# Rotary swap on VectorE instead of TensorE, and the first norm's root taken out of the projections' input

## The chip, the cores and the metric

The kernel runs on one core of one Trainium2 chip. The metric is the device time of one launch in microseconds (us). Before the change three runs took 2022.5, 2027.2 and 2033.6 us; the median, 2027.2 us, is the time before.

## The reference, cut to what matters

Two transformer blocks are computed on 512 tokens of width 1024 in fp32. What bears on the change:

```python
def rmsnorm(x, g):
    y = xf * lax.rsqrt(jnp.mean(xf * xf, axis=-1, keepdims=True) + NORM_EPS)
    return y * g
...
rot = jnp.concatenate([x1 * cos - x2 * sin, x2 * cos + x1 * sin], axis=-1)      # apply_rope
...
xn = rmsnorm(x, norm_mix_g[l])                                                  # the first norm
proj = jnp.einsum('bsd,de->bse', xn, w_in[l])
q_lat, kv_lat, k_rope, dq, dk, dv, gate_pre = jnp.split(proj, split_idx, axis=-1)
...                       # latents normed and projected up, rope on q_pe, k_pe, dq, dk; two attentions
gates = jax.nn.sigmoid(gate_pre + b_gate[l])
merged = (g_mla * jnp.einsum('bse,ed->bsd', o_mla, w_branch_mla[l])
          + g_diff * jnp.einsum('bse,ed->bsd', o_diff, w_branch_diff[l]))
```

After that come an output projection and a gated feed-forward network of hidden width 2816, then the second block: feed-forward, a mixer with two more attentions (its own rope on dq, dk, iq, ik), feed-forward.

## The kernel before

Activations lie feature-major: a tile is 128 features (partitions) by 512 tokens. `X` holds the 8 tiles of the residual. All large weights come from memory as one stream of 311 chunks of 128x1024 fp32 values. SyncE loads chunk n into `RAW[n % 3]`, ScalarE (ACT) rounds it to `HI` (`split_hi`, L967), VectorE (DVE) subtracts to get `LO` (`split_lo`, L1357), and TensorE (PE) multiplies with the pairs (`split_product`, L379 to L381): for each block of 128 features three matmuls, high by high, high by low and low by high. One chunk is thus 24 matmuls of 512 columns. ACT may split chunk n+3 only when chunk n is used, so two chunks are ready ahead of PE.

Each engine runs its own program, written by hand, and waits on semaphores. The order in an engine's program is the order in the code: in step j of a projection PE multiplies chunk j, ACT and DVE first split chunk j+2 and then do what belongs to step j. There is no planner.

The parts that the change touches:

- The start. `norm(0)` needs all of `X`: squares (ACT, L981) are summed (DVE, L1392), PE sums over partitions with matmuls against ones (`norm_sums`, L424 and L428), ACT takes the root, DVE inverts and spreads it, PE transposes it into PSUM bank 6 (`norm_spread`, L447). Then for each tile DVE scales (`scaled`, L1445), ACT rounds to `XH` (L1006) and DVE subtracts to `XL` (L1457). `behind` lets PE multiply the first two chunks tile by tile as these come. `keep_warm` (L395) runs matmuls of no use before and between.
- `project_in1`, 14 chunks: 3 tiles of q latents (`LATQ`), 2 of kv latents (`LATK`), `KR`, 4 of `DQ`, 4 of `DK`. ACT copies each out of PSUM (L1067). Two small norms of the latents run between (`norm_sums(1)` ahead of chunk 5, `norm_spread(1)` ahead of 7, `norm_sums(2)` ahead of 8, `norm_spread(2)` ahead of 11). DVE also makes the angles of the rotary tables (`angles`, L1478 to L1484).
- Rotary. For a tile, `rotate` (L462) is an fp32 matmul with a signed permutation matrix from `SQC`, which swaps the halves; DVE multiplies that by sine (L1522), the tile by cosine (L1524) and adds (L1539). There are 18: 9 in `project_in1`, 2 with the `uq` and `uk` chunks, 7 in `project_in2` (one of them `rotate_misc`).
- After `project_in1` PE waits until all 14 tiles are copied (`all_released`) and multiplies the 4 chunks `dv1`, then differential attention, `uq`, `uk`, `uv`, the second attention.
- `merge(0)`: for each of 8 output tiles two gate chunks and one branch chunk. ACT takes the sigmoid of the gates from PSUM (L1220). In the first step DVE normalizes the differential output (`diff_norm`, L1807 and L1811), PE transposes both attention outputs (`turn`, L774), ACT rounds and DVE subtracts them (L1766, L1762).

Of the kernel before, what the change touches and what calls it, by code (L numbers as in the profile page):

```python
# [7 lines left out]
F32 = mybir.dt.float32  # L8
# [7 lines left out]
P = 128  # L16
# [27 lines left out]
SQUARES = ("ident", "ones", "halves", "rot_a", "rot_p", "rot_i", "rot_m", "causal", "chunked")  # L44
NSQ = len(SQUARES)

# [16 lines left out]
def build(nc, wst, ada, xT, cols_d, squares_d, pos1_d, pos2_d, lams_d, out):  # L63
    ctx = ExitStack()
    with ctx:
# [18 lines left out]
        WARM = [(4, 1, 2), None, None, (1, 1, 2), (1, 1, 1), (1, 1, 2), (1, 1, 2)]  # L84
# [25 lines left out]
        SM2 = at("SM2", 206.5, [P, 48])  # L110
        A0 = 118
# [83 lines left out]
        FSTD, FR, FV = SM3[:, 0:8], SM3[:, 8:16], SM3[:, 16:24]  # L195
        G_BOTH = SM2[:, 40:48]
# [10 lines left out]
        NTB = np.cumsum([0] + [n[0] for n in NORMS]).tolist()  # L207
        SAB = np.cumsum([0] + [n[0] - 1 for n in NORMS]).tolist()
# [31 lines left out]
        ROT_BASE = {"in1": 0, "uq": len(ROT1), "in2": len(ROT1) + 2}  # L240
        rot_src = {}
# [64 lines left out]
        def _(pool):  # L306
            pool.dma_start(T[:, 0, :].bitcast(I32), pos1_d.partition_broadcast(P)).then_inc(sem("pos_loaded"), 16)
# [51 lines left out]
        def _(pe):  # L359
# [31 lines left out]

            def keep_warm(n):
# [46 lines left out]
            def norm_spread(k):  # L439

                pe.wait_ge(sem("expanded"), k + 1)
                if k:

                    pe.wait_ge(sem("normed"), NTB[k])
# [19 lines left out]
            def token_major(n0, nchunks, tiles_per, width, moving, banks, rotations):  # L464


                for j in range(nchunks):
                    w = chunk(n0 + j, 0, 0)
                    for b in range(NB):
                        if j == 0 and b == 2:  # L470
                            pe.wait_ge(sem("rot_read"), rotations)
# [27 lines left out]
            def project_in2():  # L499
# [31 lines left out]
                def rotation(k):  # L531
                    q = ROT_BASE["in2"] + ROT2.index(k)
                    if IN2[k][0] == "rope":
                        pe.wait_ge(sem("in_copied"), e0 + k + 1)
                    else:
                        pe.wait_ge(sem("hnormed"), NRM2.index(k) + 1)

                    if q > ROT_BASE["in2"]:
                        pe.wait_ge(sem("rot_read"), q)
                    if q == ROT_BASE["in2"] + 2:  # L540
                        pe.wait_ge(sem("values_copied"), 1)
                    rotate(q, IN2[k][1], "rot_m" if IN2[k][0] == "misc" else IN2[k][3], 5)

                def turn_values():

                    pe.wait_ge(sem("in_copied"), e0 + 3)
                    pe.wait_ge(sem("rot_read"), ROT_BASE["in2"] + 2)
# [5 lines left out]
                for j in range(IN2_STEPS):  # L553
# [7 lines left out]
                    turning = [k for k in ROT2 if rot_at(IN2, k) == j]  # L561
                    if turning:
                        amid[4] = lambda: rotation(turning[0])
# [8 lines left out]
                    if j == len(IN2):  # L572

                        pe.wait_ge(sem("in_copied"), e0 + len(IN2))
                        pe.wait_ge(sem("rot_read"), ROT_BASE["in2"] + len(ROT2))
# [50 lines left out]
            def project_in1():  # L626

                n0 = FIRST["in1"]
                for j in range(len(IN1) + 2):
                    if j - 2 in ROT1:  # L630
                        q = ROT1.index(j - 2)
                        pe.wait_ge(sem("in_copied"), j - 1)
                        if q >= 2:
                            pe.wait_ge(sem("rot_read"), q - 1)
                        rotate(q, IN1[j - 2][1], IN1[j - 2][3], 4 + q % 2)
# [8 lines left out]
                    if j == 0:  # L644
                        behind(0, n0, (0, 1))
                    elif 2 <= j < len(IN1):
# [3 lines left out]
                        used(split_product(PS[:, j % 4, :], w, range(8), range(8), (XH, XL)))  # L650
                released["in_copied"] += len(IN1)
# [232 lines left out]
            pe.wait_ge(sem("squares_loaded"), 16)  # L884
            norm(0)
            project_in1()
            all_released()

            pe.wait_ge(sem("normed"), NTB[3])
            token_major(FIRST["dv1"], 4, 2, 512, (XH, XL), DV_BANKS, len(ROT1))  # L890
# [14 lines left out]
            for m in range(4):  # L905
# [3 lines left out]
                if m in (1, 2):  # L909
                    r = m - 1  # L910
                    pe.wait_ge(sem("proj_copied"), 5 + r)
                    rotate(ROT_BASE["uq"] + r, Y[:, r, :], "rot_p", 6 + r)
            used(ins)
            token_major(FIRST["uv"], 1, 2, 512, (LKH, LKL), UV_BANKS, ROT_BASE["uq"] + 2)
# [35 lines left out]
        def _(act):  # L950
# [51 lines left out]
            def high(k, t):  # L1002
                g, oh = NORMS[k][3:5]
                act.wait_ge(sem("normed"), NTB[k] + t + 1)
# [26 lines left out]
            def token_copies(n0, nchunks, dest, width, banks):  # L1031
# [7 lines left out]
                for b in range(NB):  # L1039
                    A(dest[:, b, :], PS[:, banks[b], 0:width], ACT.Copy).then_inc(sem("v_copied"), 1)  # L1040
# [1127 lines left out]
```

## Time and profile before

| | |
|---|---|
| runs timed | 2022.5, 2027.2, 2033.6 us |
| profiled execution | span 2022.8 us from first to last instruction; its page has no other time of its own |
| PE busy | 1987.2 us (98%) |
| DVE busy | 1001.7 us (50%) |
| ACT busy | 713.8 us (35%) |
| memory read | 204 MB, 102 GB/s over the span |
| mean granted TensorE clock | 0.991 |

Busy time of an engine is the time in which it executes something, not the time at its peak rate. A row of the timeline gives start, duration, engine, line and operation, and in brackets how long the engine sat idle before it and what ended that. The chain of waits is the path that ended last, walked back from the last instruction. An fp32 matmul of 512 columns shows as two records, one of rounded operands as one.

### The profile page before, as it was taken

The numbers are of one execution on the slowest core, as the hardware profiler recorded it, in microseconds if no ns is written. First come the engines' busy times: TensorE is split into PE (matmuls) and PEld (weight loads), VectorE is DVE, ScalarE is ACT, GpSimd is POOL, SyncE is SP. The second block draws the span as 40 slices with busy tenths as digits, with TensorE's granted clock in tenths as the row PEclk, the third lists the DMA queues.
The fourth block names the chain that finished last, engine by engine and source line by source line (L and its number), as shares of the span: only waits on it lengthen the run. The fifth ranks groups of instructions, "written<-read, shape, count | busy, mean of one in ns | idle before, by whom it ended". The sixth has DMA issues, their size and how long they took to land.

```text
span 2022.8 us, 25559 instructions
## 1 busy us (share of the span) xinstructions
PE 1987.2 (98%) x9174; PEld 1591.1 (79%) x9182; DVE 1001.7 (50%) x1525; ACT 713.8 (35%) x1210; POOL 77.9 (4%) x113
## 2 busy tenths in 40 slices
PE   6999999999999999999999999999999999999999
PEld 4866778878888888788888878767777878888887
DVE  5655654467656533543334344767834653333322
ACT  4334742233222222422232223445544433232221
POOL 0010000001111000000000010400000000000000
PEclk9998999999999999999999999999999999999999
DMA  5220114455766533233333322211111223333332
GB/s 174 82 67 11 43 63 131 131 174 194 220 205 218 171 104 104 78 105 95 102 93 102 106 83 84 74 52 53 42 42 32 94 74 106 102 93 94 103 104 93
DMA packets 57513, 207.36 MB, mean 103 GB/s; under 512 B 6448, under 2 KB 6576, under 8 KB 57440
## 3 DMA queue, kind: packets, MB, share of 16 engines
q1 hardware_dynamic: 46800, 167.94, 26.5%
q0 software_dynamic: 10640, 38.44, 6.1%
q8 instruction: 47, 0.77, 0.2%
q14 instruction: 26, 0.21, 0.0%
HBM read 204.23 MB, written 2.10 MB: 102 GB/s over the span
## 4 chain that ended last, share of the span: by engine, by line
PE 94%; DVE 3%; ACT 2%; issue 1%; DMA 1%; SPq 0%; DVEq 0%; ACTq 0%
PE PS L379 27%; PE PS L381 26%; PE PS L380 26%; PE PS L726 3%; PE PS L760 2%; PE PS L665 1%; PE PS L744 1%; PE PS L462 1%; DMA SQC<-squares 1%; PE PS L854 1%; PE PS L395 1%; PE PS L687 1%; PE PS L527 1%; PE PS L496 1%; DVE BIAS L1679 0%
## 5 line engine op out<-in xcount | busy, mean ns | idle before, releaser
L1357 DVE TENSOR_TENSOR LO<-RAW,HI 128x1024 fp32r<-128x1024 f32 x311 | 383.6, 1234 | 547.4 <-ACT HI L967 546.0
L379 PE MATMUL PS<-XH,HI 128*128 128x512 f32 x1552 | 626.5, 404 | 4.6 <-ACT GATE_F L1161 2.1
L381 PE MATMUL PS<-XH,LO 128*128 128x512 f32 x1552 | 605.8, 390 | 0.0
L380 PE MATMUL PS<-XL,HI 128*128 128x512 f32 x1552 | 605.1, 390 | 0.0
L967 ACT ACTIVATE HI<-RAW 128x1024 fp32r<-128x1024 f32 x311 | 328.1, 1056 | 558.2 <-PE PS L381 541.0
L379 PEld LDWEIGHTS PS<-XH,HI 128*128 128x128 f32 x1552 | 292.2, 188 | 82.3 <-issue 19.0
L381 PEld LDWEIGHTS PS<-XH,LO 128*128 128x128 f32 x1552 | 291.6, 188 | 62.1
L380 PEld LDWEIGHTS PS<-XL,HI 128*128 128x128 f32 x1552 | 292.3, 188 | 56.7 <-issue 2.6
L379 PE MATMUL PS<-HIDH,HI 128*128 128x512 f32 x528 | 205.4, 389 | 0.0
L380 PE MATMUL PS<-HIDL,HI 128*128 128x512 f32 x528 | 205.4, 389 | 0.0
L381 PE MATMUL PS<-HIDH,LO 128*128 128x512 f32 x528 | 205.4, 389 | 0.0
L379 PEld LDWEIGHTS PS<-HIDH,HI 128*128 128x128 f32 x528 | 99.1, 188 | 20.6
L381 PEld LDWEIGHTS PS<-HIDH,LO 128*128 128x128 f32 x528 | 99.1, 188 | 20.6
L380 PEld LDWEIGHTS PS<-HIDL,HI 128*128 128x128 f32 x528 | 99.1, 188 | 20.5
L1255 ACT ACTIVATE T<-PS 128x512 f32<-128x512 f32 x45 | 26.9, 598 | 165.4 <-PE PS L381 165.2
L1884 DVE TENSOR_TENSOR Y<-T,PS 128x512 f32<-128x512 f32 x45 | 31.0, 688 | 95.6 <-PE PS L381 95.6
L1505 DVE SCALAR_TENSOR_TENSOR ACC<-ADA,SM,ACC 128x1024 f32<-128x1024 f32 x57 | 73.0, 1281 | 10.3 <-DMA ADA<-ada 9.8
L1177 ACT ACTIVATE PT<-PS 128x128 f32<-128x128 f32 (+1 forms) x96 | 42.1, 438 | 83.8 <-PE PS L744 83.7
L1730 DVE TENSOR_REDUCE SM<-PS 128x1 f32<-128x128 f32 (+1 forms) x96 | 46.8, 489 | 32.1 <-PE PS L731 12.3
L1187 ACT ACTIVATE P<-PS,SM 128x128 f32<-128x128 f32 (+1 forms) x96 | 50.5, 526 | 25.0 <-DVE SM L1730 24.1
L316 POOL DMA_DIRECT2D ADA<-ada x70 | 36.9, 528 | 526.9 <-DVE ACC L1503 252.6
L379 PE MATMUL PS<-OTH,HI 128*128 128x512 f32 x128 | 50.1, 391 | 0.4 <-DVE OTL L1762 0.4
(323 smaller groups left out, 2085.2 us busy)
## 6 DMA issues: line engine op xcount, KB each, us to landing
RAW<-weights SPq DMA_DIRECT2D x311, 512.0 KB, 3.5
ADA<-ada POOLq DMA_DIRECT2D x72, 512.0 KB, 4.5
X<-x_in SPq DMA_DIRECT2D x4, 512.0 KB, 8.5
y_out<-X SPq DMA_DIRECT2D x8, 256.0 KB, 4.7
SQC<-squares SPq DMA_DIRECT2D x1, 576.0 KB, 11.9
T<-positions POOLq DMA_DIRECT2D x1, 256.0 KB, 5.7
POS<-positions POOLq DMA_DIRECT2D x1, 256.0 KB, 3.5
LAMS<-lambdas POOLq DMA_DIRECT2D x1, 128.0 KB, 7.0
```

What stands on the lines that cost most here:

```text
L316: pool.dma_start(ADA[j][:], ada[2 * i + (j + 2)]).then_inc(sem(f"ada{j}"), 16)
L379: mm(bank, a, moving[0][:, t, :], start=start, stop=False)
L380: mm(bank, a, moving[1][:, t, :], start=False, stop=False)
L381: ins = mm(bank, z, moving[0][:, t, :], start=False, stop=stop)
L726: mm(PS[:, u % 3, 0:n], at_["q"](h, i), at_["k"](h, n), start=True, stop=False)
L760: ins = mm(PS[:, 5 + v % 2, 0:at_["dv"]], at_["PT"][v % 2][:, kb * P:(kb + 1) * P], at_["v"](kb, h), start=kb == 0, stop=kb == i)
L967: A(HI[n0 % 3][:], RAW[n0 % 3][:], ACT.Copy).then_inc(sem("hi_ready"), 1)
L1177: A(at_["PT"][v % 2][:, 0:n], PS[:, 3 + v % 2, 0:n], ACT.Copy).then_inc(sem("pt_copied"), 1)
L1187: A(at_["P"][u % 3][:, 0:n], PS[:, u % 3, 0:n], ACT.Exp, bias=NMX[:, u % 4:u % 4 + 1], accum_out=RSU[:, u % 4:u % 4 + 1]).then_inc(sem("pr ...
L1357: V.tensor_tensor(LO[n0 % 3][:], RAW[n0 % 3][:], HI[n0 % 3][:].bitcast(F32), ALU.subtract)\
L1505: V.scalar_tensor_tensor(out=ACC[:], in0=ADA[j][:], scalar=CND[:, kt:kt + 1], in1=ACC[:], op0=ALU.mult, op1=ALU.add).then_inc(sem("ada_add ...
L1730: V.tensor_reduce(NMX[:, u % 4:u % 4 + 1], PS[:, u % 3, 0:n], AX, ALU.max, negate=True)\
```

## The change

Three things change.

1. Rotary swap. The permutation matmul goes. DVE's `stream_shuffle` swaps lanes within each group of 32 partitions, from SBUF to SBUF; the sign is in the sine table now (`_freq`). A rope on DVE is thus four operations for three, and its first one reads the copied tile, no longer PSUM. The four permutation matrices leave `SQC`, which shrinks from 9 to 5 squares; `R0` takes their place in SBUF.
2. First norm. `XH` and `XL` are made from `X` times the gain, without the root. The squares follow, the sums are taken by PE after the first two chunks and the root is spread after chunk 2. DVE copies it to `R0`, and multiplies each tile by it as it takes the tile out of PSUM, which ACT did before. The `dv1` rows are scaled in ACT's copy (`NR0`). In `merge(0)` DVE multiplies each gate tile by `R0`, and ACT takes the sigmoid of that. `lambdas`, a handful of small DVE operations, moves from ahead of the projection to its step 3.
3. Loads. SyncE issues `X` and the first three chunks in turns, then `SQC`; GpSimd waits for the last part of `X` before it issues its own. `warm_up` runs five matmuls on a cleared tile at the start, and the seven useless matmuls of norm 0 go.

```diff
-        WARM = [(4, 1, 2), None, None, (1, 1, 2), (1, 1, 1), (1, 1, 2), (1, 1, 2)]
+        WARM = [None, None, None, (1, 1, 2), (1, 1, 1), (1, 1, 2), (1, 1, 2)]
@@ sync
             for t in range(4):
                 sp.dma_start(X[:, 2 * t:2 * t + 2, :], xT[:, 2 * t:2 * t + 2, :]).then_inc(sem(f"x_loaded{t}"), 16)
+                if t < 3:
+                    sp.dma_start(RAW[t][:], wst[t]).then_inc(sem(f"raw{t}"), 16)
             sp.dma_start(SQC[:], squares_d).then_inc(sem("squares_loaded"), 16)
-            for j in range(3):
-                sp.dma_start(RAW[j][:], wst[j]).then_inc(sem(f"raw{j}"), 16)
@@ gpsimd
+            pool.wait_ge(sem("x_loaded3"), 16)
@@ tensor
-            def rotate(q, src, perm, bank):
-                mm(PS[:, bank, :], SQV[perm], src, start=True, stop=True).then_inc(sem("rot_mm"), 1)
...
                     if j == 0:
                         behind(0, n0, (0, 1))
+                        pe.wait_ge(sem("squares_loaded"), 16)
+                        norm_sums(0)
...
+                    if j == 2:
+                        norm_spread(0)
@@ scalar
+                A(XH[:, t, :], X[:, t, :], ACT.Copy, scale=col("g_mix", t)).then_inc(sem("split_hi"), 1)
+                if t in (1, 3):
+                    split_hi(t // 2 - 2)
+            for t in range(DT):
                 square(0, t)
-            split_hi(-2)
-            split_hi(-1)
-            norm(0, first=DT)
             project_in1()
@@ vector, rope
-                v.wait_ge(sem("rot_mm"), q + 1)
-                ins = V.tensor_tensor(T[rows, 0, :], PS[rows, bank, :], tab[rows, 1, :], ALU.mult)
-                ins.then_inc(sem("rot_read"), 1)
-                link(V.tensor_tensor(T[rows, 1, :], dst[rows, :], tab[rows, 0, :], ALU.mult))
-                return T
+                V.stream_shuffle(T[rows, 0, :], src[rows, :], SWAP[swap]).then_inc(sem("swapped"), 1)
+                swaps[0] += 1
+                link(V.tensor_tensor(T[rows, 1, :], src[rows, :], tab[rows, 0, :], ALU.mult))
+                v.wait_ge(sem("swapped"), swaps[0])
+                link(V.tensor_tensor(T[rows, 0, :], T[rows, 0, :], tab[rows, 1, :], ALU.mult))
@@ vector, project_in1
+                    if j == 0:
+                        roots_of(0)
+                    if j == 1:
+                        v.wait_ge(sem("rstd"), 1)
+                        V.tensor_copy(R0[:], PS[:, 6, :]).then_inc(sem("normed"), 1)
+                        v.wait_ge(sem("normed"), 1)
+                    if 1 <= j <= len(IN1):
+                        v.wait_ge(sem("chunk_used"), n0 + j)
+                        kind = IN1[j - 1]
+                        V.scalar_tensor_tensor(out=kind[1], in0=PS[:, (j - 1) % 4, :],
+                                               scalar=kind[4] if len(kind) > 4 else 1.0, in1=R0[:], op0=ALU.mult,
+                                               op1=ALU.mult).then_inc(sem("in_copied"), 1)
+                    if j == 3:
+                        lambdas()
@@ vector, merge
                             split_lo(n0 + 3 * j + g, 6, i)
+                            v.wait_ge(sem("chunk_used"), 6 * i + (n0 + 3 * j + g + 1))
+                            V.tensor_tensor(T[:, g, :], PS[:, 4 * j + g, :], R0[:], ALU.mult)\
+                                .then_inc(sem("gate_raw"), 1)
                         if isinstance(i, int) and j == 0:
                             diff_norm()
```

How the order moves on DVE in one step of `project_in1`, the one that rotates the first tile of `DQ` (step 8). Before:

```order
L1357 TENSOR_TENSOR LO_59<-RAW_53,HI_56 128x1024 [waits hi_ready]
L1522 TENSOR_TENSOR T<-PS,TAB_A_83 128x512 [waits rot_mm]
L1524 TENSOR_TENSOR T<-DQ,TAB_A_83 128x512
L1539 TENSOR_TENSOR DQ<-T 128x512 [waits rot_read,dve_link]
L1445 SCALAR_TENSOR_TENSOR Y<-LATQ,CO,PS 128x512 [waits split_hi,split_lo,rstd,rotated]
L1457 TENSOR_TENSOR LQL<-Y,LQH 128x512 [waits split_hi]
```

And after:

```order
L1340 TENSOR_TENSOR LO_59<-RAW_53,HI_56 128x1024 [waits hi_ready]
L1526 SCALAR_TENSOR_TENSOR DQ<-PS,R_75 128x512 [waits chunk_used]
L1506 STREAM_SHUFFLE T<-DQ 128x512 [waits in_copied]
L1508 TENSOR_TENSOR T<-DQ,TAB_A_84 128x512
L1510 TENSOR_TENSOR T<-T,TAB_A_84 128x512 [waits swapped,dve_link]
L1538 TENSOR_TENSOR DQ<-T 128x512 [waits dve_link]
L1429 SCALAR_TENSOR_TENSOR Y<-LATQ,CO,PS 128x512 [waits split_hi,split_lo,rstd,rotated]
L1441 TENSOR_TENSOR LQL<-Y,LQH 128x512 [waits split_hi]
```

The step gains the copy out of PSUM (L1526) and the shuffle (L1506); the copy waits for a chunk, and what follows stands behind it.

On DVE early in `project_in1`, after the change, from the split of chunk 3 to the split of chunk 4 (`R_75` is `R0`; before the change only the first row, the cast and the angles stand there):

```order
L1340 TENSOR_TENSOR LO_58<-RAW_52,HI_55 128x1024 [waits hi_ready]
L1521 COPY R_75<-PS 128x512 [waits rstd]
L1526 SCALAR_TENSOR_TENSOR LATQ<-PS,R_75 128x512 [waits chunk_used,normed]
L1559 CAST T<-T 128x512 [waits pos_loaded]
L1463 TENSOR_SCALAR Y<-T,CO 128x512 [waits dve_link]
L1464 TENSOR_SCALAR RB<-Y 128x512 [waits dve_link]
L1465 TENSOR_SCALAR RB<-RB 128x512 [waits dve_link]
L1467 SCALAR_TENSOR_TENSOR Y<-RB,Y 128x512 [waits dve_link] x3
L1469 TENSOR_SCALAR Y<-Y 128x512 [waits dve_link]
L1340 TENSOR_TENSOR LO_59<-RAW_53,HI_56 128x1024 [waits hi_ready]
```

The angles and the split of chunk 4 now stand behind a wait for the root (`rstd`), which PE spreads after chunk 2.

On DVE at the start of `merge(0)` before (`OTL` takes the low part of the turned attention outputs):

```order
L1357 TENSOR_TENSOR LO_59<-RAW_53,HI_56 128x1024 [waits hi_ready,g_sub_scaled]
L1357 TENSOR_TENSOR LO_60<-RAW_54,HI_57 128x1024 [waits hi_ready]
L1807 RECIPROCAL SM<-SM 128x16 [waits diff_std]
L1811 TENSOR_SCALAR OD<-OD,SM 128x128 [waits dve_link]
L1811 TENSOR_SCALAR OD<-OD,SM 128x128 x15
L1766 TENSOR_TENSOR OTL_101<-PS,OTH_100 128x512 [waits turned_hi] x4
```

And after:

```order
L1340 TENSOR_TENSOR LO_59<-RAW_53,HI_56 128x1024 [waits hi_ready,g_sub_scaled]
L1786 TENSOR_TENSOR T<-PS,R_75 128x512 [waits chunk_used]
L1340 TENSOR_TENSOR LO_60<-RAW_54,HI_57 128x1024 [waits hi_ready]
L1786 TENSOR_TENSOR T<-PS,R_75 128x512 [waits chunk_used]
L1817 RECIPROCAL SM<-SM 128x16 [waits diff_std]
L1821 TENSOR_SCALAR OD<-OD,SM 128x128 [waits dve_link]
L1821 TENSOR_SCALAR OD<-OD,SM 128x128 x15
L1773 TENSOR_TENSOR OTL_102<-PS,OTH_101 128x512 [waits turned_hi] x4
```

The normalization of the differential output stands behind both gate chunks now.

## Rows read from the trace of the kernel before

**Rows 1.** The page, busy time and share of each engine.
```profile
PE 1987.2 (98%) x9174; PEld 1591.1 (79%) x9182; DVE 1001.7 (50%) x1525; ACT 713.8 (35%) x1210; POOL 77.9 (4%) x113
```

**Rows 2.** The page, chain that ended last, shares by engine.
```profile
PE 94%; DVE 3%; ACT 2%; issue 1%; DMA 1%; SPq 0%; DVEq 0%; ACTq 0%
```

**Rows 3.** Timeline of the start: start us, duration us, engine, line, operation.
```profile
14.46 1.15 ACT L981 ACTIVATE SQ<-X 128x512 f32<-128x512 f32 x2 [1.41 <-DMA X<-x_in]
15.75 5.18 PE L395 MATMUL PS<-SQC 128*128 128x512 f32 x8 [15.75 <-DMA SQC<-squares]
...
18.28 1.06 ACT L967 ACTIVATE HI<-RAW 128x1024 fp32r<-128x1024 f32 x1 [0.21 <-DMA RAW<-weights]
...
26.61 0.47 PE L379 MATMUL PS<-XH,HI 128*128 128x512 f32 x1 [0.60 <-DVE XL L1457]
...
38.59 0.50 PE L379 MATMUL PS<-XH,HI 128*128 128x512 f32 x1 [0.32 <-DVE LO L1357]
```

**Rows 4.** The page, DMA issues: size of one, median us to landing.
```profile
RAW<-weights SPq DMA_DIRECT2D x311, 512.0 KB, 3.5
```

**Rows 5.** Chain of waits in the first projection: start us, us, what.
```profile
55.21 0.79 PE PS L424 x8
55.99 0.89 PE PS L428 x8
...
67.88 0.86 PE PS L462 x2
68.74 0.44 PE PS L447 x4
...
116.76 0.23 PE PS L479
```

**Rows 6.** Timeline of DVE, one step of the first projection.
```profile
103.93 1.23 DVE L1357 TENSOR_TENSOR LO<-RAW,HI 128x1024 fp32r<-128x1024 f32 x1 [3.43 <-ACT HI L967]
105.08 0.68 DVE L1522 TENSOR_TENSOR T<-PS,TAB_A 128x512 f32<-128x512 f32 x1
105.68 0.68 DVE L1524 TENSOR_TENSOR T<-DK,TAB_A 128x512 f32<-128x512 f32 x1
106.39 0.69 DVE L1539 TENSOR_TENSOR DK<-T 128x512 f32<-128x512 f32 x1
107.12 0.75 DVE L1445 SCALAR_TENSOR_TENSOR Y<-LATK,CO,PS 128x512 f32<-128x512 f32 x1
108.57 0.69 DVE L1457 TENSOR_TENSOR LKL<-Y,LKH 128x512 fp32r<-128x512 f32 x1 [0.70 <-ACT LKH L1006]
```

**Rows 7.** Timeline of DVE: lambdas, cast and angles, squares added.
```profile
36.02 0.22 DVE L1964 TENSOR_TENSOR LAMS<-LAMS 128x64 f32<-128x64 f32 x1
...
37.05 0.23 DVE L1970 CAST CAUSAL_B<-SQC 128x128 bf16<-128x128 f32 x1
...
40.35 0.42 DVE L1548 CAST T<-T 128x512 f32<-128x512 int32 x1
...
44.42 0.43 DVE L1484 TENSOR_SCALAR Y<-Y 128x512 f32<-128x512 f32 x1
...
53.43 1.42 DVE L1392 TENSOR_TENSOR RB<-RB,SQ 128x512 f32<-128x512 f32 x2
```

**Rows 8.** Timeline at the start of the merge, DVE and PE.
```profile
275.56 3.22 DVE L1811 TENSOR_SCALAR OD<-OD,SM 128x128 f32<-128x128 f32 x16
...
279.12 2.48 DVE L1766 TENSOR_TENSOR OTL<-PS,OTH 128x512 fp32r<-128x512 f32 x4 [0.33 <-ACT OTH L1202]
279.87 2.45 PE L774 MATMUL PS<-SQC,OD 128*128 128x128 f32 x16 [0.25 <-DVE OTL L1766]
...
285.45 0.50 PE L379 MATMUL PS<-OTH,HI 128*128 128x512 f32 x1 [0.38 <-DVE OTL L1762]
```

**Rows 9.** Stretches: busy us of PE, PEld, DVE, ACT, POOL, granted clock, DMA.
```profile
150.00:153.00 3.00, 3.00 (x14) 2.21 (x13) 2.29 (x9) 1.72 (x5) 0.00 (x0) 0.50 0.01 3
...
452.30:455.70 3.40, 3.34 (x8) 1.92 (x8) 2.15 (x4) 1.26 (x2) 0.00 (x0) 0.50 0.00 0
```

More of the change, by code:

```diff
@@ L42, with swapped @@
 NCOLS = _at
-SQUARES = ("ident", "ones", "halves", "rot_a", "rot_p", "rot_i", "rot_m", "causal", "chunked")
+SQUARES = ("ident", "ones", "halves", "causal", "chunked")
 NSQ = len(SQUARES)
+def swapped(half):
+    return [p + half if p < half else p - half if p < 2 * half else p for p in range(32)]
+SWAP = {"rot_a": swapped(8), "rot_p": swapped(16), "rot_i": swapped(4)}
 STREAM = (("in1", 14), ("dv1", 4), ("uq", 3), ("uk", 1), ("uv", 1), ("merge1", 24), ("out1", 8),
@@ L207, in build @@
         NTB = np.cumsum([0] + [n[0] for n in NORMS]).tolist()
+        NDB = np.cumsum([0, 1] + [n[0] for n in NORMS[1:]]).tolist()
         SAB = np.cumsum([0] + [n[0] - 1 for n in NORMS]).tolist()
@@ L390, in used, with warm_up @@
                 ins.then_inc(sem("chunk_used"), 1)
+            def warm_up(n):
+                pe.wait_ge(sem("warm_set"), 1)
+                for _ in range(n):
+                    mm(PS[:, 5, :], Y[:, 1, 0:P], Y[:, 1, :], start=True, stop=True)
             def keep_warm(n):
@@ L628, in project_in1 @@
                 n0 = FIRST["in1"]
[L629 to L635, printed above, removed]
+                for j in range(len(IN1)):
                     if j == 5:
@@ L1062, in project_in1 @@
                 n0 = FIRST["in1"]
-                for j, kind in enumerate(IN1):
+                for j in range(len(IN1)):
                     split_hi(n0 + j)
+                    if j == 0:
+                        stds(0)
                     latents(j)
-                    act.wait_ge(sem("chunk_used"), n0 + j + 1)
-                    A(kind[1], PS[:, j % 4, :], ACT.Copy, scale=kind[4] if len(kind) > 4 else 1.0)\
-                        .then_inc(sem("in_copied"), 1)
             def project_in2():
@@ L1541, in project_in1, with lambdas @@
                     latents(j)
+            def lambdas():
+                v.wait_ge(sem("lams_loaded"), 16)
+                for j in range(2):
+                    link(V.tensor_tensor(LAMS[:, 256 + 64 * j:320 + 64 * j], LAMS[:, 128 * j:128 * j + 64],
+                                         LAMS[:, 128 * j + 64:128 * j + 128], ALU.mult))
+                    V.tensor_reduce(LAM[:, j:j + 1], LAMS[:, 256 + 64 * j:320 + 64 * j], AX, ALU.add)\
+                        .then_inc(sem("lams_used"), 1)
+                v.wait_ge(sem("squares_loaded"), 16)
+                link(V.tensor_copy(IDENT_B[:], SQV["ident"]))
+                link(V.tensor_copy(CAUSAL_B[:], SQV["causal"]))
+                v.wait_ge(sem("cond_ready"), 1)
             def latents(j):
@@ L2097, in _freq @@
         if p % period < rot:
-            col[p] = f[p % period % half]
+            col[p] = -f[p % period] if p % period < half else f[p % period - half]
     return col
@@ L2134, in _squares @@
     q[:64, n["halves"], :64] = q[64:, n["halves"], 64:] = 1.0
-    for name, spans in (("rot_a", [(0, 8), (64, 8)]), ("rot_p", [(32 * b, 16) for b in range(4)]),
-                        ("rot_i", [(32 * b, 4) for b in range(4)]), ("rot_m", [(0, 8), (64, 4)])):
-        for first, half in spans:
-            for r in range(first, first + half):
-                q[r + half, n[name], r] = -1.0
-                q[r, n[name], r + half] = 1.0
     q[:, n["causal"], :] = np.triu(np.full((P, P), NEG, np.float32), 1)
```

119 lines of the change are left out of this document (45 added, 74 removed).

## Prediction

> **What bounds the kernel now.** I read the shares of busy time first: PE is busy 98% of the span, DVE half of it [rows 1]. The chain of waits agrees: 94% of it is PE [rows 2]. So a change pays where it takes work off PE or lets PE start sooner, and costs where it makes PE wait for DVE. Three stretches of the timeline then matter. At the start PE does nothing before 15.75 us, when the squares land, then useless matmuls and the norm; its first product starts at 26.61, after all of X, the norm and the scaling of tile 0, and chunk 2 starts at 38.59 [rows 3]. In the first projection PE never stands still: three chunks take 55.21 - 38.59 = 16.6 us, 5.54 each; a norm's sums take 0.79 + 0.89 = 1.7, its spread 0.44, a rotation 0.86 on the chain [rows 3, 5]. DVE has 3.4 us of idle ahead of its split there [rows 6]. At the start of the merge PE waits for DVE already, by a few tenths [rows 8].
>
> **The start.** Before, X has landed by 14.46 and the second chunk by 18.28, with GpSimd's loads sharing the way [rows 3]. Between those two SyncE moved the squares and two chunks, so 512 KB take about 1.27 us when nothing shares. One chunk takes 3.5 us from issue to landing [rows 4]; issued at about 1.3, the first part of X lands near 5, and three more pieces, the last of them chunk 1, near 8.8. Its high part takes ACT 1.06, its low part DVE 1.23: PE starts its first product at about 11.3 instead of 26.61, which is 15.3 us sooner. X is complete at 12.6 and its last low tile near 15, while PE, with 48 matmuls at 0.23, needs that tile only at 21: the two chunks take 11.1 us. The squares and their sums (seven additions at 0.71, [rows 7]) end near 20, under those products. The warm-up matmuls lie in the wait for data.
>
> **The first projection.** PE's own time: 11.1 + 12 chunks x 5.54 = 66.5, + three sums 5.0 + three spreads 1.3 = 83.9. The nine rotations (7.7) are gone. On DVE each step gains a copy out of PSUM, 0.67 start to start for an operation of 0.75, as L1445 is [rows 6], and the shuffle. No row has a shuffle. The fastest 128x512 operation on DVE takes 0.42 (the cast, [rows 7]), the ordinary two-operand one 0.69 [rows 6]; the dearest, twice as wide, 1.23. I bound the shuffle by 0.43 and by 1.38, twice the ordinary one, and take 0.69, the row it is nearest to: a full pass over 128x512. The rope is then 0.61 + 0.72 x 3 = 2.77, with one wait on its own result more.
>
> The waits of PE for DVE, in order:
> - Chunk 4. DVE gets the root when PE begins chunk 3. Then R0 0.69, copy 0.75, cast and angles 4.5 (40.35 to 44.85, [rows 7]), split 1.23: 7.2 against 5.54. Wait 1.7.
> - Sums of norm 1. Two copies 1.34, two splits 2.3, lambdas 1.26 (36.02 to 37.28), a copy 0.67, a clear 0.5, two additions 1.42: 7.5 against 5.54. Wait 1.95.
> - Sums of norm 2. From the end of chunk 6: 0.2, high part 1.06, split 1.15, copy 0.67, rope 2.77, clear and addition 1.25: 7.1 against a spread and a chunk, 6.0. Wait 1.1.
> - Spread of norm 2. Three steps with latents of 1.15 + 0.67 + 2.77 + 0.75 + 0.70 + 0.69 = 6.7 (the last two with the hop over ACT, [rows 6]), the second held by its chunk, and the third with 0.6 for the root: 21.6 against 1.7 + 16.6. Wait 3.3.
> - After chunk 13 PE waits for all 14 copies, which are now behind DVE's ropes: 21.5 against 0.44 + 16.6. Wait 4.5. ACT did these copies right behind the chunk before.
>
> Together 12.6. `dv1` starts at 11.3 + 83.9 + 12.6 = 107.8 instead of 116.76 [rows 5]: -9.0 us. So the 23 us that the loads and the rotations give are cut to 9 by DVE.
>
> **The rest.** In `uq` and `uk` two rotations go, -1.7; DVE's ropes there get longer, but the attention's first softmax waits for ACT's copies of the values, which move forward with PE, so I cost them at nothing (2 x 0.7 if that cover is gone). Merge: the normalization began at 275.3, before the gate chunks ended at 277.9. Now it starts behind the second gate's multiplication, at 277.9 + 0.69 = 278.6, ends 3.5 later at 282.1, and the first low tile is there at 282.8 where it was at 279.8 [rows 8]: +3.0, and nothing behind it catches up. The other gate multiplications (16 x 0.69) lie in DVE's idle time, and the longer way to the sigmoid, +0.7, has two chunks of 5.54 ahead of it. Second projection: seven rotations, -6.0. `rotate_misc` gets two shuffles for a step that is already DVE's longest; I give back 1.3 for it (between 0 and 3): -4.7.
>
> Sum without the clock: -9.0 - 1.7 + 3.0 - 4.7 = -12.4 us.
>
> **The clock.** The granted clock was 0.50, the level of 1.2 GHz, in the first half of the differential attention and again for 3.4 us at 452.3, right after the sums of a norm with their waits and one-column matmuls [rows 9]. Such a drop costs 3.4 / 2 = 1.7 us when PE is the bound. The change makes PE stand still where it never did: some 3 us between the warm-up and the first product, 2 us next to the sums of norm 1, 3.3 at the spread of norm 2, 4.5 before `dv1`, 3 in the merge. I count three drops: +5.1. The bounds are none and five (+8.5). The Trainium skill (TensorE: Matmul & The Clock Gate, "Why this matters for your kernels") advises against idle gaps between bursts because the clock falls back; that speaks against this change, and the 0.50 behind the quiet stretches agrees with it.
>
> The forecast is -12.4 + 5.1 = -7.3: a span of 2015.5 against 2022.8. The profiled execution lies near the fastest timed run, 4.4 below the median; from the median it is 2027.2 - 7.3 = 2019.9 us.
>
> The Trainium skill (VectorE: DVE Perf Modes, "The perf-mode tier table (the rule you actually need)") gives the shuffle only the plain rate, about 2400 ns for 2048 elements against 2293 ns for an fp32 tensor_tensor. No row here shows it; by it the shuffle would be an estimated 0.8 us, and the sum 1 us worse.
>
> **Rivals.**
> - *PE stays at 2.4 GHz.* The idle gaps are short and each is broken by a few matmuls; before, gaps of 0.2 to 0.6 us left no mark in [rows 3]. But the merge of idle and one-column matmuls did cost the clock at 452. Time 2027.2 - 12.4 = 2014.8, and 2012.5 with a shuffle of 0.43.
> - *DVE keeps up.* If the waits of 12.6 + 1.3 are not there, and the clock holds, the gain is 12.4 + 13.9 = 26: 2001. For it: DVE is 50% busy [rows 1]. Against it: that is a mean; in these steps it has 6.7 to 7.2 us of work in 5.5.
> - *More drops and a dearer DVE.* Five drops and a shuffle of 1.38: 0.69 more in some nine places that gate PE (seven steps of the projection, two ropes or the misc step later), +6.2, and +3.4: 2029.5, no change.
> - *The shuffle is slow, and the kernel slower.* If lanes cross at a quarter of the ordinary rate, one takes 2.76, 2.07 more. Every step from 7 to 13 is then DVE's, as are both ropes before the second attention and the misc step: 11 x 2.07 = +22.8, together 2042.7. It turns the gain into a loss from a shuffle of 0.69 + 7.3 / 11 = 1.35 on, and by over 0.5% from 2.3 on. Against it: it is a copy with one source, and all of DVE's 128x512 rows lie between 0.42 and 0.75 [rows 6, 7].
>
> **How the numbers follow.** A difference below 0.5%, 10 us, can't be told from none here; the three runs before spread by 11. Chances: forecast (2016 to 2025) 0.45; clock holds 0.30; DVE keeps up 0.07; more drops and a dearer DVE 0.12; slow shuffle 0.06. Faster by over 0.5% is below 2017.1: the clock that holds, DVE that keeps up and a little of the forecast's own range, 0.40. Slower by over 0.5%, above 2037.3, is most of the last, 0.05. Same 0.55. The range runs from 2010 (no drops, the shuffle at 0.43, waits a few us shorter) to 2030 (the third rival).
>
> **What would show it.** The first product near 11.3; a shuffle near 0.7; PE idle in five places of the first projection released by DVE, the last the largest, and `dv1` near 108; about 3 us of idle for OTL in the merge; no L462; new stretches at 0.50. The prediction is wrong if PE doesn't wait for DVE ahead of `dv1`, if the shuffle costs more than 1.4, or if chunk 1 lands after 11.

## The result, and the profile after

| | before | after |
|---|---|---|
| median (range) of the runs, us | 2025.32 (2022.46 to 2037.16, 11 runs) | 2045.87 (2034.87 to 2052.20, 10 runs); 2047.24 with an eleventh of 7197.57 |
| ratio, 95% interval | | 1.0078 [1.0054, 1.0102] |
| profiled execution: span, mean granted clock | 2022.8, 0.991 | 2045.2, 0.975 |

The change makes the kernel slower: by 0.8% or 16 us by the ratio in the table, by 20.5 us by the two medians, where 7 us less were forecast. The run of 7197.57 us is left out of both. The page after, to hold beside [rows 1], and below it the granted clock in 40 slices:

```profile
PE 2001.5 (98%) x9134; PEld 1604.0 (78%) x9142; DVE 1030.8 (50%) x1587; ACT 708.8 (35%) x1196; POOL 78.0 (4%) x113
...
PEclk9885999999999999999999999999999999999999
```

PE has 40 operations fewer and is busy 14 us longer. That can't be work; the last line says what it is: slices 2 to 4, 51 to 204 us, have a lower clock.

The start and the first projection on PE, beside [rows 3, 5] (start us, us, what, and in brackets the idle time before it and its releaser):

```profile
1.87 7.07 PE L406 MATMUL PS<-Y 128*128 128x512 f32 x10 [1.87 <-DVE Y L1966]
12.24 0.47 PE L389 MATMUL PS<-XH,HI 128*128 128x512 f32 x1 [3.30 <-DVE LO L1340]
...
45.54 1.05 PE L440 MATMUL PS<-SQC,RB 128*128 128x1 f32 x8 [1.62 <-DVE RB L1375]
...
67.24 1.05 PE L440 MATMUL PS<-SQC,RB 128*128 128x1 f32 x8 [1.18 <-DVE RB L1375]
...
92.38 1.09 PE L463 MATMUL PS<-SQC,RB 128*128 128x128 f32 x4 [3.54 <-DVE Y L1429]
...
115.54 0.50 PE L490 MATMUL PS<-HI,XH 128*128 128x512 f32 x1 [4.64 <-DVE DK L1526]
```

The rows at 12.24, 45.54, 67.24, 92.38 and 115.54 are the first product, the sums of norms 1 and 2, the spread of norm 2 and `dv1`. The first product starts at 12.24 instead of 26.61, `dv1` at 115.54 instead of 116.76: of 14.4 us won, 13.2 are gone 103 us later. The waits of PE in this stretch (us in total, times, longest):

```profile
PE PS L389 <- DVE LO L1340: 4.9, 2, 3.3
PE PS L490 <- DVE DK L1526: 4.6, 1, 4.6
PE PS L463 <- DVE Y L1429: 3.5, 1, 3.5
PE PS L440 <- DVE RB L1375: 2.8, 2, 1.6
```

4.9 is the 3.3 ahead of the first product and 1.6 ahead of chunk 4. One step of DVE, beside [rows 6]:

```profile
102.42 0.68 DVE L1526 SCALAR_TENSOR_TENSOR DK<-PS,R 128x512 f32<-128x512 f32 x1
103.03 0.01 DVE L1506 LOAD_MASK_SELECT T<-DK  x1
103.03 0.74 DVE L1506 STREAM_SHUFFLE T<-DK 128x512 f32<-128x512 f32 x1
103.65 0.67 DVE L1508 TENSOR_TENSOR T<-DK,TAB_A 128x512 f32<-128x512 f32 x1
104.36 0.69 DVE L1510 TENSOR_TENSOR T<-T,TAB_A 128x512 f32<-128x512 f32 x1
```

The shuffle is an ordinary pass: 0.74, 0.62 from start to start. Now the stretches of PE, to hold beside [rows 9] (busy us and count, granted clock, DMA share, GB/s):

```profile
48.00:51.00 3.00, 3.00 (x9) 0.50 0.56 175
69.00:75.00 6.00, 6.00 (x17) 0.50 0.30 87
93.00:96.00 3.00, 3.00 (x10) 0.55 0.03 5
...
117.00:120.00 3.00, 3.00 (x10) 0.57 0.00 0
120.00:143.00 23.00, 22.52 (x99) 1.00 0.29 92
145.00:160.00 15.00, 15.00 (x44) 0.50 0.00 0
160.00:180.00 20.00, 20.00 (x57) 0.50 0.00 1
180.00:200.00 20.00, 20.00 (x62) 0.55 0.00 0
```

The kernel before, in one of these:

```profile
160.00:180.00 20.00, 19.67 (x103) 1.00 0.00 0
```

Each of the four gaps shown from 45 us on comes with a stretch at 0.50, the level of 1.2 GHz, that begins at the gap's end or within 3 us of it: 3.4 us, 6.8, 3.4 and 3.4. In differential attention the clock is at 0.50 from 143.5 for 54.6 us, where it was there for 17. In the same 20 us PE runs 57 instructions instead of 103, and reads as fully busy in both: the busy share doesn't show the low clock. Over the whole trace 105.3 us lie at 0.50, against 37.0.

The second attention and the merge, beside [rows 8]:

```profile
235.09 0.46 PE L718 MATMUL PS<-KM,QM 96*128 96x128 f32 x2 [2.38 <-DVE QM L1996]
...
299.29 2.47 DVE L1773 TENSOR_TENSOR OTL<-PS,OTH 128x512 fp32r<-128x512 f32 x4
300.03 3.42 PE L766 MATMUL PS<-SQC,OD 128*128 128x128 f32 x16 [3.05 <-DVE OTL L1773]
...
303.10 0.78 PE L389 MATMUL PS<-OTH,HI 128*128 128x512 f32 x1
```

Before, these stood at 217.84, 279.12, 279.87 and 282.07. So the difference of the two traces is -14.4 at the first product, -1.2 at `dv1`, +17.3 at the second attention, +21.0 at the merge's first product and +22.4 at the end.

### The profile page after: what moved, and what is told of

The parts are those of the page before. It is cut to its first block and busy times, and to the rows that moved or that the text cites. A ratio compares the mean times of both kernels' runs of the same rounds, so it can differ in the third digit from the quotient of the medians.

```text
span 2045.2 us, 25500 instructions
## 1 busy us (share of the span) xinstructions
PE 2001.5 (98%) x9134; PEld 1604.0 (78%) x9142; DVE 1030.8 (50%) x1587; ACT 708.8 (35%) x1196; POOL 78.0 (4%) x113
## 5 line engine op out<-in xcount | busy, mean ns | idle before, releaser
L391 PEld LDWEIGHTS PS<-HIDH,LO 128*128 128x128 f32 x528 | 99.1, 188 | 20.4
L1243 ACT ACTIVATE HIDH<-Y 128x512 f32 (+1 forms) x66 | 41.7, 631 | 25.8 <-DVE Y L1894 25.8
```

What stands on the lines that cost most here:

```text
L391: ins = mm(bank, z, moving[0][:, t, :], start=False, stop=stop)
L1243: A(HIDH[:, bass.ds(t, 1), :], Y[:, 0:1, :], ACT.Copy).then_inc(sem("hid_hi"), 1)
```

## The experiments

Two theories. **A**: the loss is the clock: PE's gaps, and the stages behind them, put PE at 1.2 GHz for longer. **B**: the loss is the waits for DVE and the shuffle itself. Each execution gives a time and a mean granted clock, and within one kernel they lie on a line: for 128 executions of the kernel before, 1.74 us per 0.001 of clock, for the others 1.1 to 2.0. So each result is read in two numbers, the median clock and the time on the kernel's own line at a clock of 0.985. The second is the work and the waits, the first what A is about. The runs of some kernels don't reach 0.985: those of after and a_again end at 0.982, those of r_release at 0.983, and those of f_before begin at 0.990; there the last column extends the line. The ratios with their intervals are those given with the runs, and not the quotients of the medians. Each version has 9 to 12 runs, f_after only 6.

| kernel | median us | ratio to before, interval | median clock | at 0.985 |
|---|---|---|---|---|
| before (all runs) | 2027.1 | | 0.991 | 2036.7 |
| after | 2045.9 | 1.0078 [1.0054, 1.0102] | 0.976 | 2029.6 |
| a_again | 2042.7 | 1.0062 [1.0032, 1.0092] | 0.978 | 2029.1 |
| k1_shuffle_only | 2034.6 | 1.0030 [1.0009, 1.0050] | 0.986 | 2035.4 |
| f_before | 2035.3 | 1.0033 [1.0016, 1.0051] | 0.992 | 2043.8 |
| f_after | 2045.8 | 1.0084 [1.0057, 1.0111] | 0.983 | 2042.8 |
| o1_order | 2024.2 | 0.9985 [0.9960, 1.0009] | 0.985 | 2023.4 |
| o_order_again | 2025.9 | 0.9977 [0.9944, 1.0010] | 0.984 | 2024.1 |
| g_gaps | 2035.5 | 1.0028 [1.0003, 1.0053] | 0.983 | 2030.6 |
| r_release | 2036.4 | 1.0044 [1.0019, 1.0068] | 0.981 | 2028.6 |
| p_perope | 2028.1 | 1.0006 [0.9972, 1.0040] | 0.987 | 2029.9 |
| g_order_gaps | 2023.0 | 0.9978 [0.9951, 1.0004] | 0.986 | 2023.7 |
| d_gap_before | 2038.3 | 1.0064 [1.0033, 1.0095] | 0.987 | 2043.9 |
| e_filled_gap | 2036.4 | 1.0049 [1.0021, 1.0076] | 0.991 | 2045.6 |
| h_light_fill | 2021.7 | 0.9966 [0.9941, 0.9991] | 0.989 | 2030.3 |
| h_fill_after | 2036.8 | 1.0034 [1.0008, 1.0060] | 0.985 | 2036.0 |
| q_best | 2027.5 | 0.9982 [0.9955, 1.0010] | 0.986 | 2028.6 |
| p_order | 2021.2 | 0.9958 [0.9933, 0.9983] | 0.987 | 2025.2 |
| p_order_again | 2017.7 | 0.9928 [0.9898, 0.9958] | 0.990 | 2025.3 |

The first three lines decide it: at one clock the changed kernel is 7 us faster than the one before, and its clock is lower by 0.013 to 0.015, which by the 1.74 is 23 to 26 us. Where both have runs the difference is of that size too: at a clock of 0.981 and 0.982 the kernel before took 2043.0 to 2043.9 us, the changed one 2033.6 to 2036.8.

**One part alone.** k1_shuffle_only is the kernel before with only the rotations changed:

```
-    rotate(q, IN1[j - 2][1], IN1[j - 2][3], 4 + q % 2)       # TensorE
+    V.stream_shuffle(T[rows, 0, :], src[rows, :], SWAP[swap]) # VectorE
```

> The kernel before with the rotary swap on DVE alone; norm, loads and ACT's copies out of PSUM stay. Clock theory (the change loses by stretches at 1.2 GHz that its gaps on PE bring): 18 rotations of 0.86 us are gone (-15.5), DVE gives back 8 to 10 in waits, mostly in the two projections; the sum is -5 to -7 us if the cold stretches stay as before, and up to +10 if the long cold stretch of the differential attention comes with it. Rival (the shuffle on DVE is itself what costs): slower than before by 5 us or more, with PE idle for DVE making up the difference and a cold time like before's 37 us.

Taking PE's rotations away makes the kernel slower by 6 to 7 us, although at one clock it is 1.3 us faster. So of the 15.5 us of work taken from PE some 14 come back, more than the 8 to 10 expected: waits eat the gain, as B says. That a loss comes of it is the clock, 0.986 for 0.991. The time lies in the range of both theories; what tells them apart is the time at 0.50, which the rival put at the 37 us of before. In the profiled execution it is 56.7: 3.4, 3.4 and 6.8 us from the first projection to the start of `dv1`, and 13.7 in differential attention. The long stretch there isn't needed for a loss.

**The reverse.** p_perope is the changed kernel with the swap of the first projection and of `uq` back on PE, with the root on eviction, loading, merge and the second projection's shuffle kept:

```
-    rope(dst, IN1[j - 2][2], IN1[j - 2][3])
+    rope_mm(q, 4 + q % 2, dst, IN1[j - 2][2])   # reads rotate()'s bank
```

> The changed kernel with the swap of the first projection and of uq back on TensorE (fp32 matmul against a permutation, as in the kernel before, eleven of them of 0.86 us), with root on eviction, warm-up, alternate loading, merge and the shuffle of the second projection kept. VectorE is relieved of 11 shuffles of 0.72 us, TensorE gets 9.5 us of work back. Theory A: the gaps of the first projection go, and the clock stays up: the first product is 14.4 us earlier than before, the rest is as before plus 3 for the merge and 3 for the second projection, less its 6 swaps: 2012 to 2022. Theory B (the shuffle is cheap, the loss is in the other parts: evictions with the root on VectorE, merge): 2040 or more.

It gives 9.5 us of PE work back, and its time at one clock stays where it was (2029.9 for 2029.1 to 2029.6): the rotations cost PE nothing that it didn't lose waiting for DVE's shuffles. The clock rises by about 0.01, and the median falls by 14.5 to 18 us. It missed the 2012 to 2022 expected; three of its twelve runs, at 2044 to 2046, still have the changed kernel's median clock, 0.976 and 0.977.

**A gap on purpose.** d_gap_before adds nothing of the change to the kernel before but a wait of PE ahead of `dv1`; e_filled_gap puts useless matmuls into the same gap:

```
     project_in1()
+    for _ in range(10):                    # e_filled_gap only
+        mm(PS[:, 3, :], SQV["ident"], SQC[:, 0:4, :].rearrange("p n m -> p (n m)"), ...)
+    pe.wait_ge(sem("idled"), 6)            # six useless VectorE operations
```

> The kernel before with nothing of the change, but with a gap made on purpose: TensorE waits ahead of dv1 until VectorE has done six useless multiplications of 128x512 after the last rotation (about 5 to 6 us idle on TensorE, the place where the changed kernel waits 4.6). Theory A (a gap costs itself and lowers the clock behind it): +5.5 for the gap and 3 to 55 us more at 0.50, at 0.45 each: 2033 to 2050, with granted clocks of 0.975 to 0.985. Theory B (a gap costs itself alone): 2031, clock 0.99 as before.

> The kernel before with the same six useless VectorE operations that TensorE waits for ahead of dv1, but with ten useless fp32 matmuls of 128x512 put into the gap (it was 9.2 us, they are 8.6 us at the full clock). The time that TensorE loses to the gap is the same, only it isn't idle in it. Theory A (idle gaps lower the clock): the granted clock goes back to the 0.991 of the kernel before, and the time to about 2027 + 8 = 2035 with its best runs at 2031, the mean clock 0.004 above that of the idle gap. Theory B (a gap is only lost time): no difference from the idle gap, 2038 and a clock of 0.987.

The gap was 9.2 us, more than intended. PE ahead of `dv1` and three stretches around it, with the gap idle:

```profile
125.87 0.80 PE L479 MATMUL PS<-HI,XH 128*128 128x512 f32 x1 [9.22 <-DVE T L1975]
```
```profile
112.00:121.00 9.00, 4.65 (x17) 1.00 0.19 58
121.00:127.00 6.00, 1.13 (x3) 0.50 0.00 0
127.00:131.00 4.00, 4.00 (x11) 0.50 0.41 131
```

And with the gap filled:

```profile
112.00:121.00 9.00, 9.00 (x32) 1.00 0.17 58
121.00:127.00 6.00, 6.00 (x15) 1.00 0.00 0
127.00:131.00 4.00, 3.36 (x15) 1.00 0.22 56
```

This pair shows the mechanism in the rows of one execution each: the idle gap brings a drop of 10.2 us that begins in it and goes on over the first work behind it; with work in the gap there is none. In differential attention, too, the first has 34.1 us at 0.50 and the second 13.7. In whole executions the pair is weaker. The median clock is 0.987 against 0.991 as A expects, but both kernels keep their spread (2035 to 2054 and 2034 to 2053), and rank tests of 9 against 12 runs leave them undecided (p = 0.2 for the times, 0.1 for the clocks; p is the chance that runs of one and the same kernel would part at least that far). Most of the cost of either is the 7 to 9 us of the gap.

**The gaps of the changed kernel.** g_gaps fills them, r_release shortens one:

```
+    keep_warm({4: 1, 5: 1, 8: 1, 11: 3}.get(j, 0))   # g_gaps; also warm_up(7), and 5 ahead of dv1
```
```
-    all_released()                                   # r_release: ahead of dv1
+    pe.wait_ge(sem("in_copied"), 12)
```

> The changed kernel with useless fp32 matmuls (128x512 from the constants, 0.86 us each at the full clock, into bank 5, which nobody reads) put ahead of the six waits of TensorE: 2 more in the warm-up ahead of the first product, 1 ahead of chunk 4, 1 ahead of each of the two sums of squares, 3 ahead of the spread of norm 2, 5 ahead of dv1. They are meant to fill gaps that exist anyway. Theory A (the loss is the clock: gaps in the first projection drop it there, and the stage after them starts from a low level): the stretches at 0.50 before 125 us go (17 us of them, about 0.45 us each, -7 us); if the 54.6 us stretch of differential attention goes too, another -16: 2024 to 2031, else about 2040. Theory B (the loss is the waits themselves and the shuffle): 2047, or up to 2050, since nothing waits less.

> The changed kernel, but dv1 starts when 12 of the 14 evictions of the first projection are done and not all 14 (its first banks are 3 and 6, so the two last tiles need not be out). The 4.6 us wait ahead of dv1 shrinks to what the gain of norm 2 leaves, about 2 to 3 us. Theory A: if this gap decides whether differential attention runs at the low clock, 2030 to 2035; if the long stretch comes by other reasons, 2045. Theory B: 2045 (-2).

> The changed kernel once more, on the chip and in the rounds of the next three, since a step of 17 or 54 us at the low clock in differential attention seems to be drawn anew in each execution. If the draw is the kernel's own: median 2044 to 2050 again, most runs at a granted clock of 0.972 to 0.978. If it was the hour or the chip: 2036 like the version with the earlier dv1.

a_again shows that after's time is its own, though its median of 2042.7 is a little below the 2044 expected: 19 runs on two occasions have a median of 2044.5. Filling the gaps makes nothing earlier (2030.6 at one clock), yet gives 9 us (p = 0.001 against those 19), by the clock. That is short of the 2024 to 2031 of A: in the profiled execution 3.4 + 3.4 us at 0.50 are left ahead of `dv1` where 17 were, and 37.5 in differential attention. r_release takes 1.9 us from one wait, 1 us at one clock, and gives 8 (p = 0.006); its 2036.4 lies between the 2030 to 2035 and the 2045 expected. In its profiled execution `dv1` was again followed by 3.4 us at 0.50, but differential attention came back to the full clock:

```profile
160.00:180.00 20.00, 19.67 (x100) 1.00 0.00 1
```

Six of its twelve runs have a clock of 0.982 or 0.983, the others 0.974 to 0.979. The clocks of g_gaps are spread as widely, 0.977 to 0.987. So less idle time ahead raises the clock over many runs. It doesn't decide the long stretch in one: o1_order below has the same short wait ahead of `dv1`, and 54.6 us in its profiled execution; o_order_again, the same kernel, has 13.7.

**Work in differential attention.** In this stage PE waits in each of 16 steps for the combined probabilities. A filler ahead of that wait, 128x512 in f_before and f_after, 128x256 in h_fill_after and h_light_fill:

```
+    mm(PS[:, 3 + w % 2, :], SQV["ident"], SQC[:, 0:4, :].rearrange("p n m -> p (n m)"), ...)
     pe.wait_ge(sem("combined"), w + 1)
```

> The kernel before with 16 fp32 matmuls of no use (512 columns, 0.86 us each at full clock) in the differential attention, each ahead of PE's wait for the combined probabilities. Clock theory: PE has more to do there, the level 0.50 ends after the first steps or doesn't come, and the stage takes no longer than before (-5 to +2 us in all), with less spread between runs. Rival (the stage is bound by its chain of softmax steps, not by the clock): +5 to +14 us.

> The changed kernel with the same 16 matmuls. Clock theory: the 54.6 us at 0.50 shrink to under 20, the time falls by 8 to 16 us against the changed kernel, to 2030 to 2038. Rival (DVE's waits carry the loss): no gain, +5 to +14 us.

> The changed kernel with one useless fp32 matmul of 128x256 (0.43 us) in each of the 16 steps of differential attention, nothing else. If the state of that stage is what the changed kernel loses by: the stretch of 54.6 us goes, clock 0.983 to 0.986, at +6.6 for the filler: 2034 to 2038 against 2044. If the clock is lost elsewhere: 2050.

The big filler missed both expectations of the clock theory. f_before takes 8 us more where -5 to +2 were expected, which is the rival's range: at a clock of 0.992, where both kernels have runs, 2035.8 for 2025.3, so it costs 10.5 us, and there is little to win back (the 7 by the table's last column is the extended line). f_after takes 2045.8 where 2030 to 2038 were expected. The stretch of 54.6 us does shrink to 10.2 in its trace, but the filler costs 13 us at one clock, about as much as the clock gives back. The small one costs 6.7 and gives 14 by the clock (0.0075 above that of the 19 runs): all twelve runs of h_fill_after lie at a clock of 0.982 to 0.986, 2034 to 2041, and in the same window as above it reads

```profile
160.00:180.00 20.00, 20.00 (x100) 1.00 0.00 1
```

The expectation of 2034 to 2038 held. So work put into this stage alone wins back 14 of the 23 to 26 us that the clock takes. In this trace the stage still has 13.7 us at 0.50, and 20.4 us lie ahead of it.

**Fewer waits.** o1_order changes only the order: the angles ahead of the wait for the root, the lambdas in the last step, `dv1` after 12 evictions, and

```
     split_lo(n0 + 3 * j + g, 6, i)
+    if isinstance(i, int) and j == 0 and g == 0:
+        diff_norm()                          # was behind the gate's multiplication
```

> The changed kernel with DVE's order mended: angles ahead of the wait for the root, lambdas behind the ropes, dv1 waits for 12 copies, the output's normalization ahead of the gate multiplications. By the gaps alone about 7 us of PE's waits go (1.7 + 1.9 + 1.8 + 2). Clock theory: fewer gaps also bring fewer drops, so -7 to -15 us against the changed kernel, and the long stretch at 0.50 may or may not go. Rival (only the waits count): -7, with the same cold time.

> The reordered version with shuffles everywhere, unchanged, once more: 2022 to 2028 with a few runs at 2036 to 2042. At one and the same granted clock it should lie 2 us below the one with TensorE's swap, and its median clock below that one's.

At one clock it gains 6 us on the changed kernel, near the 7 expected of the waits, and the clock rises by 0.007: 18 to 20 us in all, beyond the 7 to 15 expected. The repetition held to its 2022 to 2028, and lies 1 us below the version with TensorE's swap at one clock, not 2. 5 of its 24 runs in all still have a time of 2035 or more. With filled gaps, and with these and the small filler:

> The reordered kernel (angles ahead of the wait for the root, lambdas last, dv1 after 12 evictions, the merge's norm ahead of its first multiplications; 2024 us) with useless matmuls in the gaps that it still has: 2 in the warm-up, 1 ahead of the sums of norm 2, 3 ahead of the spread of norm 2, 2 ahead of dv1. Theory A: drops before dv1 go (-3 to -5) and the runs at 2036 to 2042 get rarer: median 2015 to 2022. Theory B: 2024 to 2027.

> The reordered kernel with filled gaps (2023.0), and in each of the 16 steps of differential attention one more useless fp32 matmul of 128x256 ahead of the wait for the combined probabilities (0.43 us at the full clock, half the size of the filler that cost 10 us in the kernel before). Theory A: the stretch at 0.50 in this stage shrinks from 17 or 55 us to 10 or less, which gives 3 to 20 and costs up to 16 x 0.43 = 7 where the stage waits less than that: 2015 to 2022, and a narrower spread. Theory B: +7, 2030.

They lie 1 to 4 us below it. The 2023.0 of g_order_gaps decides nothing between 2015 to 2022 and 2024 to 2027. The 2021.7 of h_light_fill is within A's range; its filler costs 6.6 at one clock and gives a little more, 8.

**The best version.** p_order joins the two that pay: PE's swap where DVE is what PE waits for (first projection and `uq`), and the order of o1_order. q_best adds two warm-up matmuls and a filler of 128x128.

> The version with the swap of the first projection and of uq on TensorE, and the reordered waits too (angles early, lambdas last, dv1 after 12 evictions, the merge's norm ahead of its first multiplications). Against the same without the order (2028.1): the merge gives 2, chunk 4 and the norm sums 2 to 3. Theory A: 2020 to 2024, and no better than the reordered one with shuffles and filled gaps (2023.0), since 9.5 us of TensorE work are back. Theory B (the shuffle was the harm): 2015.

> The version with TensorE's swap in the first projection and uq and reordered waits (2021.2), with 2 more matmuls in the warm-up and one of 128x128 (0.22 us, 3.4 us in all) in each of the 16 steps of differential attention. Theory A: the stretch of 37 us in that stage shortens, 2015 to 2020, at a clock of 0.988 to 0.991. Theory B: 2024.

> The version with TensorE's swap in the first projection and uq and reordered waits, unchanged, once more. If its gain is real: median 2019 to 2024, ratio 0.995 to 0.998. If it was a lucky draw of the clock: 2025 and a ratio with 1 inside its interval, as with the version with added fillers (2027.5).

p_order beats the kernel before twice, by 0.4% and 0.7%, and with it the changed one; the first time as expected, the second below the 2019 to 2024 said. Its 22 runs have a median of 2020.4 against 2025.4 for the 24 of the version with shuffles everywhere (p = 0.0001), although at one clock it is 1.5 us slower: it wins by its clock, 0.988 for 0.984. Three of its waits for DVE in the first 320 us, the longest and those of the merge and of `dv1`:

```profile
PE PS L391 <- DVE LO L1358: 3.9, 1, 3.9
...
PE PS L781 <- DVE OTL L1796: 1.0, 1, 1.0
PE PS L480 <- DVE DK L1547: 0.6, 1, 0.6
```

The wait ahead of `dv1` is 0.6 where it was 4.6, that of the merge 1.0 where it was 3.1. In differential attention the two profiled executions still have 37.5 and 30.7 us at 0.50. q_best was a miss: 3.4 us later at one clock, about the 3.5 of its 16 fillers, and its clock is no better.

## Why the prediction was wrong

**What held.** The waits of PE for DVE in the first projection came out as worked out: 1.6, 1.62, 1.18, 3.54 and 4.64 are 12.6, and 1.7, 1.95, 1.1, 3.3 and 4.5 were said, with the same releasers. Singly they are off by up to 0.33; that the errors cancel in the sum is luck. None of the three signs that were to prove the prediction wrong came. The shuffle was taken at 0.69 (0.8 by its other estimate) and is 0.72 to 0.76. The merge's wait was put at 3.0 and is 3.05. The first product came 0.9 late (12.24 for 11.3), behind two `XL` operations on DVE that the estimate of its chunk's low part had not put ahead of it. Two readings were loose without harm: of the 14 us that "DVE" cuts from 23, 12.6 are waits, and most of the rest is the first norm's sums and spread, which now stand behind the first product; and a timed run is 2.0 us longer than its span (2047.24 for 2045.2), so the profiled execution before lay some 2.4 and not 4.4 us below the median.

**The step that failed** is the clock: "I count three drops: +5.1", with five as the bound (+8.5). The trace has four drops up to the first products of `dv1` alone, 3.4 + 6.8 + 3.4 + 3.4 = 17 us, then 54.6 us in place of 17 in differential attention, and 68 us more at 0.50 in all. Half of that is 34 us where PE is the bound; the experiments' lines give 23 to 26. Two errors are in the step. It took the length of one drop, 3.4 us, for the length of all, although [rows 9] show a clock of 0.50 through the whole of 150 to 153. And it counted only gaps, as if a stage's own low clock couldn't last longer than before. The time, 2045.9 us, lies beyond the end of the range at 2030. By the two traces:

| stretch | predicted | measured | what made it up |
|---|---|---|---|
| to `dv1` | -9.0 | -1.2 | first product +0.9; drops of 13.6 us, half of it 6.8 |
| `dv1` to second attention | -1.7 | +18.5 | drops of 3.4 at 117 and 54.6 for 17.1; wait of 2.38 for the ropes |
| to the merge's first product | +3.0 | +3.8 | wait 3.05; its transposes at the low clock, 3.42 for 2.45 |
| the rest | -4.7 | +1.4 | waits for the ropes; some 7 us more at 0.50 |

The first line closes to 0.1: -9.0 + 0.9 + 6.8 = -1.3. The second doesn't: -1.7 + 1.7 + 18.8 + 2.4 are 21.2, 2.7 more than measured. Half of the time at 0.50 is too much for this stage, where PE also waits: its waits for DVE's `P` fell from 2.2 us to 1.3.

**Two covers that were not there.** The ropes of `uq` were costed at nothing, with 1.4 if the cover is gone. The second attention starts 2.38 after a wait for them: PE reaches it before DVE has done both. In the second projection I gave back 1.3 for DVE; PE waits there 2.6 for `QF` and 2.2 for `DQ`, 4.8 in all, beyond the bound of 3:

```profile
PE PS L527 <- DVE QF L1590: 2.6, 1, 2.6
...
PE PS L527 <- DVE DQ L1594: 2.2, 2, 1.8
```

These are 2.4 and 3.5 more than forecast, 5.9 us, somewhat more than the 4.8 to 5.3 between -12.4 and the -7.1 to -7.6 at one clock. They belong to the shuffle: k1_shuffle_only, which changes nothing else, has the waits of 2.4 for `QM`, 2.6 for `QF` and 2.1 for `DQ`, and in p_perope, with the swap of `uq` back on PE, the one for `QM` is gone.

**The rivals.** "PE stays at 2.4 GHz" rested on the gaps being short; but the one of 1.62 us at 45.5 is followed by a drop. "More drops and a dearer DVE" had the mechanism, with five drops, and its price was a third of what came. "DVE keeps up" is refuted by the 12.6 us of waits. The slow shuffle is refuted by its row, though its time of 2042.7 is near the result: the right time for a wrong reason. The Trainium skill's advice against idle gaps (TensorE: Matmul & The Clock Gate, "Why this matters for your kernels") agrees with the idle gap of 9.2 us and the filled one above; the gaps of 1.2 and 1.6 us that had a drop behind them here are shorter than those it warns of. It stood in the prediction with too small a price.

**What stays open.** Why one and the same kernel, as o1_order and o_order_again, has 13.7 us at 0.50 in differential attention in one execution and 54.6 in another. The odds move with the gaps ahead and with the work in the stage; what draws the single case no run here shows. Nor was it tried what the merge and the alternate loading are worth alone.

## What to carry to other kernels

Work that is moved off a saturated TensorE is a gain only if nothing makes TensorE wait in its place: first sum up each step of the engine that takes it over. Where that step is longer than TensorE's, as 7 us against 5.5 here, leave the work. Price a new gap by what the stages behind it lose at the low clock, by the longest such stretch in the trace and not the shortest, above all ahead of a stage of many small matmuls and waits. And compare versions by time and granted clock over ten executions or more: single executions of the unchanged kernel differ by 24 us here.

## What the runs showed of the hardware

- The granted clock fell behind idle gaps of TensorE of 1.2 and 1.6 us next to one-column matmuls, in a first projection otherwise dense. Two others, 1.6 us ahead of chunk 4 and 3.3 ahead of the first product, have no drop behind them in this trace. In that of a_again, the same kernel, the one ahead of the first product is 4.4 us and the clock falls in it, for 3.4 us; its first matmul takes 0.77 us for 0.47. The long stretches at 0.50 in the traces are of 30.7, 34.1, 37.5 and 54.6 us, all in differential attention.
- Executions of one kernel fall into groups: 128 of the kernel before lie at 2022.5 (clock 0.993), 2025 (0.991 and 0.992), 2030 (0.988 and 0.989), 2034 to 2037 (0.985 to 0.987) and 2043 (0.981), with three runs between or beyond these (0.980, 0.982, 0.990), and nothing at 0.983 and 0.984.
- Useless fp32 matmuls in a wait are not free: 16 of 128x256, 0.43 us each at the full clock, 6.9 us together, cost 6.6 and 6.7 us at one clock, though each stood ahead of a wait.
- An fp32 STREAM_SHUFFLE of 128x512 takes 0.72 to 0.76 us, and the LOAD_MASK_SELECT ahead of each 0.01.
